# Where the A and M operands of TensorE's matmuls begin in SBUF, in a two-layer transformer kernel

## What is computed

```python
# block 1
q, k, v, z, xbc, dt_raw = split(rms_norm(x, g_mix) @ w_in)        # 2048 x 6160
x = x + concat([dilated_attention(q, k, v), ssd_mixer(z, xbc, dt_raw)]) @ w_out
x = x + cross_attention(rms_norm(x), rms_norm(mem), w_cq, w_ckv, w_co)
x = x + square(relu(rms_norm(x, g_mlp) @ w_up)) @ w_down           # 2048 x 8192, 8192 x 2048
# block 2
xr, gr, q, k, v, qi, ki, wi, g_rnn, g_att = split(x @ w_in_2)
x = layer_norm(ALPHA * x + (sigmoid(g_rnn) * y_rnn + sigmoid(g_att) * y_att) @ w_out_2)
gate, up = split(causal_dwconv(x @ w_up_2))                        # 2048 x 11264
x = layer_norm(ALPHA * x + (silu(gate) * up) @ w_down_2)           # 5632 x 2048
```

## The kernel before, in words

| pair | jobs | matmuls |
|---|---|---|
| MH, ML | w_out_s (16 granules) | 384 |
| AH2, AL2 | w_ck (8), w_co (8), w_down (128) | 192, 192, 3072 |
| AH2, AL2, stationary | w_cv (8) | 96 |
| AH4, AL4 | w_down2 (32, 32 and 24) | 2112 |
| XH, XL | all the others | 15360 (288 of them in v and v2) |

## Time and profile before

### The profile page before, as it was taken

The page is one execution under the profiler, slowest core; times in us unless marked ns, Lnnn a source line. Parts: engine busy times, 40 slices in busy tenths (PEclk is TensorE's granted clock), DMA queues, the critical chain, the costliest instruction groups (busy, mean ns, idle before and its releaser), DMA issues.

```text
span 2760.3 us, 52761 instructions
## 1 busy us (share of the span) xinstructions
PE 2704.7 (98%) x22440; PEld 2642.9 (96%) x22440; DVE 1788.5 (65%) x2601; ACT 1339.7 (49%) x1811; POOL 111.8 (4%) x75
## 2 busy tenths in 40 slices
PE   8999999999999999999999999999899999999996
PEld 8998889899999999999899999999899999999996
DVE  6787679675555555555587786556676646664666
ACT  5464566454344443444444684444365435543543
POOL 2000021010000000000000000000400000000003
PEclk9999999999999999999999999999899999999998
DMA  6534445365555555555454456565355555555552
GB/s 241 178 136 140 160 138 176 132 208 190 187 194 185 190 191 184 192 189 179 145 170 141 164 176 203 194 193 180 125 199 192 192 184 197 192 190 185 195 186 84
DMA packets 136603, 488.45 MB, mean 177 GB/s; under 512 B 15152, under 2 KB 17584, under 8 KB 136368
## 3 DMA queue, kind: packets, MB, share of 16 engines
q1 hardware_dynamic: 136368, 485.09, 51.8%
HBM read 482.93 MB, written 2.10 MB: 176 GB/s over the span
## 4 chain that ended last, share of the span: by engine, by line
PE 96%; DVE 2%; issue 1%; ACT 1%; DMA 0%; SPq 0%; ACTq 0%; DVEq 0%
PE ps L753 95%; PE ps L756 1%; DVE T L1694 1%; DMA cst<-in_cst 0%; DVE WL L1694 0%; ACT xT L1177 0%; DVE xT L1694 0%; DVE small L1702 0%; DVE q L1694 0%; ACT P L1177 0%; DVE small L1694 0%; DVE AL L1702 0%; SPq L706 0%; ACT WH L1177 0%; DVE P L1698 0%
## 5 line engine op out<-in xcount | busy, mean ns | idle before, releaser
L1694 DVE TENSOR_TENSOR WL<-raw,WH 128x1024 fp32r<-128x1024 f32 x907 | 1121.9, 1240 | 796.5 <-ACT WH L1177 795.0
L1177 ACT ACTIVATE WH<-raw 128x1024 fp32r<-128x1024 f32 x907 | 960.4, 1059 | 1346.2 <-PE ps L753 1344.7
L753 PE MATMUL ps<-XH,WH 128*128 128x256 f32 x5024 | 1406.3, 280 | 23.7 <-issue 10.8
L753 PE MATMUL ps<-XL,WH 128*128 128x256 f32 x5024 | 1392.6, 277 | 0.0
L753 PE MATMUL ps<-XH,WL 128*128 128x256 f32 x5024 | 1392.4, 277 | 0.0
L753 PEld LDWEIGHTS ps<-XH,WH 128*128 128x128 f32 x5024 | 944.6, 188 | 31.8 <-issue 27.7
L753 PEld LDWEIGHTS ps<-XL,WH 128*128 128x128 f32 x5024 | 944.2, 188 | 2.4 <-issue 1.5
L753 PEld LDWEIGHTS ps<-XH,WL 128*128 128x128 f32 x5024 | 943.9, 188 | 0.3
L753 PE MATMUL ps<-AH,WH 128*128 128x256 f32 x1856 | 524.3, 282 | 0.2 <-DVE AL L1694 0.2
L753 PE MATMUL ps<-AL,WH 128*128 128x256 f32 x1856 | 523.2, 282 | 0.0
L753 PE MATMUL ps<-AH,WL 128*128 128x256 f32 x1856 | 521.5, 281 | 0.0
(11 more groups left out here) (227 smaller groups left out, 1645.3 us busy)
## 6 DMA issues: line engine op xcount, KB each, us to landing
raw<-in_w_up SPq DMA_DIRECT2D x304, 512.0 KB, 3.4
raw<-in_w_in SPq DMA_DIRECT2D x224, 512.0 KB, 3.5
raw<-in_w_down SPq DMA_DIRECT2D x216, 512.0 KB, 3.4
raw<-in_w_out SPq DMA_DIRECT2D x64, 512.0 KB, 3.5
raw<-in_w_gates SPq DMA_DIRECT2D x64, 512.0 KB, 4.3
raw<-in_w_ckv SPq DMA_DIRECT2D x16, 512.0 KB, 3.3
raw<-in_w_cq SPq DMA_DIRECT2D x8, 512.0 KB, 4.4
raw<-in_w_co SPq DMA_DIRECT2D x8, 512.0 KB, 3.3
```

Of the source, the lines that this page charges most:

```text
L753: return e.matmul(out, l, r, start=start, stop=True, skip_group_check=True)
L1177: return e.activation(out, x, func, **kw)
L1694: return e.tensor_tensor(out, a, b, op)
```

## The change

The argument `skip` of the six `skewed` tensors of the A and M pairs becomes 8 elements (32 bytes): it was 96 for MH and ML and 16 for the A pairs. Sizes, names, the order of instructions, the waits and the arithmetic stay; XH and XL keep 16.

```diff
             with ExitStack() as p1c:
-                MH = skewed("MH", 8, 96, p1c)
-                ML = skewed("ML", 8, 96, p1c)
+                MH = skewed("MH", 8, 8, p1c)
+                ML = skewed("ML", 8, 8, p1c)
                 memT = sb("memT", [128, 16, 256], F32, p1c)
 
         with ExitStack() as p2:
-            AH2 = skewed("AH2", 16, 16, p2)
-            AL2 = skewed("AL2", 16, 16, p2)
+            AH2 = skewed("AH2", 16, 8, p2)
+            AL2 = skewed("AL2", 16, 8, p2)
...
         with ExitStack() as p4:
-            AH4 = skewed("AH4", 16, 16, p4)
-            AL4 = skewed("AL4", 16, 16, p4)
+            AH4 = skewed("AH4", 16, 8, p4)
+            AL4 = skewed("AL4", 16, 8, p4)
```

## The result

The changed kernel takes 2735.12 us, the median of four runs (2733.32 to 2737.57); the kernel before took 2762.22 beside it. The ratio is 0.9904 with a 95% interval of 0.9886 to 0.9921: faster by 27 us, a little under 1%. The forecast was 2728.1 within 2726 to 2737, so the time lies in the range, and the gain is 7 us less than the 34 that were summed up. It lies above 2732.1, where the forecast's own terms end at their low bounds, and so in the margin beyond them. The profiled execution took 2737.57 us, the longest of the four, around a span of 2735.8; that span is 24.5 us shorter than the one before.

What follows compares the result with a forecast made beforehand. The prediction took PE, busy 98% of the span, and its matmul pace as the bound. Terms 30.0 + 1.3 + 1.1 + 0.5 + 1.4 - 0.2 gave 34.1 us, hence 2728.1 us against the median, range 2726 to 2737.

Steps and rivals of the forecast that it cites:

- The main step: In w_down and w_down2, 6.75 blocks take X's pace by operand place: 4.45 us less each, 30.0 us in all.
- Rival 1: Whole kernel: tensor region or stage sets the pace, so nothing changes; 2762.2 us, chance 0.06.
- Rival 3: A and M blocks: reversed order of slot distances puts all slots at A's worse level; 6.2 us slower, 2768.4, chance 0.03.
- Rival 2: A blocks: another distance counts too, pace only reaches 117.0 ns; gain 11.7 us, 2750.5 us, chance 0.06.
- w_co: In stage w_co, 192 matmuls go from 118.9 to 113.3 ns, a gain of 1.1 us.
- w_out_s: In stage w_out_s, 384 matmuls go from 117.0 to 113.3 ns: 1.4 us gained, between 0.7 and 1.4.
- At X's steady pace a block takes 87.04: In w_down and w_down2, 768 matmuls at 113.33 ns take 87.04 us in place of 91.49.
- 1.3 us for X blocks behind A: Six X blocks behind A blocks lose their two slow first granules, 0.21 us each; between nothing and 1.3 us.
- q2 behind a value projection: First granule of q2, behind an X job, takes 2.73 us without slow start; slow starts were therefore laid to A's pace.
- The cover: ScalarE's 1.7 us wait per granule in w_down hides the makers' writes; faster PE takes only 0.14 us of it.
- w_ck: In stage w_ck, VectorE nearly fills the time, so half the possible gain is taken: 0.5 us, between nothing and 1.1.
- w_cv: In stage w_cv, A is stationary; first pass might go from 409 to X's 419 ns, taken as a 0.2 us loss.

Runs made afterwards that it cites:

- e2_sweep: Against the changed kernel, M pair moved to 96, AH2/AL2 to 32, AH4/AL4 to 0 bytes modulo 128 from the ring; 2753.24 us.
- e3_x96: Against the changed kernel, XH and XL moved from 64 to 96 bytes modulo 128 from the ring; 2806.87 us.
- e4_all32: Against the changed kernel, a 32-byte gap ahead of WH shifts ring and everything behind it, all distances kept; 2736.95 us.
- e1_a40: Against the changed kernel, A and M skip 40 elements instead of 8, giving X's slot order modulo 256; median 2731.09 us, ratio 0.9889 to the kernel before.
- e11_again: The changed kernel itself, unaltered, run four more times beside the skip-40 version on one chip; 2735.91 us, ratio 0.9902 to the kernel before.
- e10_a40: The kernel of e1_a40 run again four times, beside the changed kernel on one chip; 2731.48 us, ratio 0.9884 to the kernel before.
- e7_finer: Against e1_a40, AH2/AL2 at 56, AH4/AL4 at 72, MH/ML at 0 bytes modulo 128 from the ring; 2769.93 us.
- e8_rest: Against e1_a40, AH2/AL2 at 112, AH4/AL4 at 16 bytes modulo 128; MH and ML at 64 in opposite slot orders; 2752.00 us.
- e9_skew0: Against e1_a40, the ring's SKEW set to 0 for all four slots instead of 0, 32, 64, 96; 2783.29 us.
- e5_split: Against e1_a40, high and low parts split: AL2 and AH4 moved to 96 bytes modulo 128, AH2 and AL4 kept at 64; 2758.48 us.

## Why the prediction was right, and where 7 us went

**The main step held, and the time was in the range by its margin.** The gain was put on a pace that goes with the operand's place and on 6.75 blocks; e2_sweep, e3_x96 and e4_all32 show that the distance from the ring sets it, and the seven blocks of w_down and w_down2 gave 26.6 us (16.5 + 8.2 + 1.9). Rival 1 (nothing changes) fell with the first w_down block. With it falls, for this kernel, what the forecast took from the Trainium skill's page "SBUF — State Buffer", section "Who interferes with whom": with two independent read ports for PE, moving X by 32 bytes (e3_x96) should cost nothing, and it cost 72 us against the change. The page says nothing of start addresses, and which accesses meet, no run here shows. Rival 3 (the order of slots counts, at the worst level) had its mechanism partly right and its price wrong: the order counts, but only for two or three granules at a boundary. Rival 2's 2750 us did not come; a pace near its 117 ns did, 117.9, but in those first granules alone. That the time lies under 2737 is in part luck: this end had been set for a step towards rival 2, and what it had to cover was something else. In the profiled execution the gains of A's w_down and w_down2 blocks (26.6 us against 28.6), of w_co (0 against 1.1) and of w_out_s (0.5 against 0.7) lie below the low bounds of their terms, and the first w_up, which had no term, costs 1.1 us.

**"At X's steady pace a block takes 87.04"** failed as the term for A's blocks: they take 87.37, since the slow start of X's blocks was read as something that A's pace leaves behind and that goes with it. It stayed, and A got one of three granules. That is 6.75 x 0.33 = 2.2 us, and the **1.3 us for X blocks behind A** came to nothing, 3.5 us together. The check that the forecast made, q2 behind a value projection, could not tell the two readings apart: there the operand before is X as well, so neither A's pace nor a turned order comes ahead of it. e1_a40, which gives A and M X's order, has the forecast's numbers: 87.04 in both kinds of block.

**The last w_down2 block** was put at three quarters of a full one, 3.3 us, and gave 1.9. The chain of the changed kernel in that block passes through VectorE:

```profile
2676.55 4.68 DVE xT L1694 x4
2682.36 3.40 DVE xT L1694 x2
2685.76 2.25 DVE WL L1694
2688.06 18.98 PE ps L753 x165
```

The `xT` pieces are layer norm's work, which lies there among the weights. Before, the chain of this stretch was PE's own; now PE waits for WL ahead of 2688.06 and loses about 0.5 us. The slow start takes another 0.3, and the rest is in granules between small matmuls, some at 117.8 ns. The cover, called free at 1.7 us a granule from a w_down stretch, was read in a stretch without that work.

**w_co and the first w_up**, put at 1.1 us and 0, gave nothing and cost 1.1 us. In the profiled execution the granted clock is low for longer behind PE's gap ahead of w_co. Stretches of the changed kernel, then of the kernel before, columns as in rows 3:

```profile
548.00:550.00 2.00, 2.00 (x9) 1.82 (x8) 0.52 (x2) 0.94 (x2) 0.00 (x0) 0.50 0.04 8
550.00:552.00 2.00, 2.00 (x11) 2.00 (x11) 2.00 (x2) 0.39 (x1) 0.00 (x0) 0.50 0.00 0
```

```profile
548.00:550.00 2.00, 2.00 (x10) 1.91 (x10) 1.20 (x2) 1.33 (x2) 0.00 (x0) 0.50 0.00 0
550.00:552.00 2.00, 2.00 (x17) 2.00 (x16) 1.49 (x2) 0.00 (x0) 0.00 (x0) 0.84 0.23 80
```

The clock is at its lower level, 1.2 GHz (0.50), from 548 to 552 us; before, it was so from 548 to 550 and rose to 2.4 GHz on the way to 552 (0.84); PE starts 11 matmuls between 550 and 552 us instead of 17, about 0.7 us lost there alone. In e11_again, the same kernel, w_co takes 23.54 us, 0.8 less than before. Then PE runs into VectorE, which makes X's low part for w_up in between:

```profile
574.83 3.67 DVE XL L1702 x4
579.70 2.27 DVE WL L1694 x2
581.97 4.16 DVE XL L1702 x4
587.41 6.25 PE ps L753 x52
```

Before, the chain from 546.7 to 591.9 us was PE throughout; now it is VectorE from 572.6 to 587.3, and the block is 1.07 us longer. It is so in e1_a40 too, with 89.06 us, and in e10_a40, with 89.08, in which w_co takes only 22.91 us. Where A has a place with a slower pace it stays short: 87.94 us in e2_sweep, 87.96 in e7_finer, and 88.75 in e8_rest, where that pace is 115.8 ns. So part of what w_co gains is lost again in the next block: a term of 1.1 us that the forecast put at nothing.

**The start** cost 1.56 us in this execution: between 22 and 24 us PE had a clock of 0.51 and 11 matmuls, before it had 1.00 and 20. No operand that was moved is in use there, and in e1_a40 w_out_s begins at 353.85 us, earlier than before. This belongs to the execution; in e11_again, the same kernel, w_out_s begins at 354.70. It can be a part of the 4 us over which the runs of one kernel spread, and of the 2.5 us by which the profiled execution lies above the median.

**w_out_s** (-0.5 against -1.4) fell short because in most of its granules small matmuls lie between the others and the pace behind them is one of the two: of its ten unbroken stretches seven have 117.8 or 117.9 ns and three 113.5 to 113.8. The 1.4 us had been put on all 384. **w_ck** came out near its term (-0.6 against -0.5), with no wait for VectorE in the trace. **w_cv** did so by luck: its first pass went from 409 to 406 ns and not to 419, its matmuls got 0.2 us shorter from first to last, and the 0.3 us are in the gap behind it, which grew by 0.5.

## What to carry to other kernels

Where each matmul loads new weights and PE has no gap, read the pace from start times by operand, over a known count, before looking for work to remove: two paces for the same instruction, changing at the operand's boundary, point to addresses, and the cure costs a few bytes of padding. Give all moved operands the same distance from the weights, here 64 modulo 128 bytes, high and low parts alike, and also the same order from slot to slot; measure it, since 8 bytes off was worse than a wrong multiple of 32. Read the cover of the other engines in each stretch where PE gets faster, not in the cleanest one.

## What the runs showed of the hardware that was not expected

- Of ten places one is good. At 64 bytes a 128x256 fp32r matmul with its weight load starts every 113.3 ns, at 56 every 119.9 and at 72 every 120.9.
- At that place two paces exist with the same distances and the same clock, 113.3 and 117.8 ns. Without the ring's skew (e9_skew0) an unbroken stream stays in the one it has for whole blocks; two small matmuls in between changed it once, at 1953.81 us. Moving the ring's slots by 128 bytes each brings it to the faster one in the runs that were made; why is open.
- One of three passes at a bad place costs 5.4 of the 5.8 ns that all three cost (e5_split: 118.7 against 119.1 and 113.3), and two cost 4.6.
